# Prompt stick-breaking attention by pairs of heads, and cache pages issued by two engines

## The reference, cut to what matters

```
z[t,s] = q_t . k_s / 8 + b_h                 for s < t, else masked
beta   = sigmoid(z);  rem = sigmoid(-z) = 1 - beta
A[t,s] = beta[t,s] * prod_{s<j<t} rem[t,j]
o[t]   = sum_s A[t,s] v_s
```

## Time and profile before

| what | us |
|---|---|
| median of 3 executions | 1375.97 (1371.51 to 1376.88) |
| the profiled execution's own time | 1370.01 |
| its span in the profile | 1368.3 |
| TensorE busy in the span | 1262.4 (92%) |
| VectorE busy | 410.7 (30%) |
| ScalarE busy | 243.7 (18%) |
| GpSimd busy | 88.7 (6%) |

### The profile page before, as it was taken

The page is one execution under the profiler, slowest core; times in us unless marked ns, Lnnn a source line. Parts: engine busy times, 40 slices in busy tenths (PEclk is TensorE's granted clock), DMA queues, the critical chain, the costliest instruction groups (busy, mean ns, idle before and its releaser), DMA issues.

```text
span 1368.3 us, 19903 instructions
## 1 busy us (share of the span) xinstructions
PE 1262.4 (92%) x7806; PEld 572.1 (42%) x7806; DVE 410.7 (30%) x944; ACT 243.7 (18%) x413; POOL 88.7 (6%) x156
## 2 busy tenths in 40 slices
PE   3999996979998999999999999999999999999996
PEld 2777774559552333333333333333333333333332
DVE  1750242364362213122123212213222223212214
ACT  2214232232221101102011011101101011011103
POOL 1600122024200000000000000000000000000000
PEclk8999998889989999999999999999999999999998
DMA  9444489600255999999999999999999999999993
GB/s 324 165 128 123 136 268 369 217 21 16 112 220 201 401 429 429 429 428 428 428 428 428 429 429 429 429 428 429 428 428 429 428 428 429 428 429 429 428 426 157
DMA packets 67031, 464.11 MB, mean 339 GB/s; under 512 B 16685, under 2 KB 16813, under 8 KB 42148
## 3 DMA queue, kind: packets, MB, share of 16 engines
q1 hardware_dynamic: 64420, 455.01, 81.4%
q0 software_dynamic: 2560, 8.39, 1.7%
HBM read 459.67 MB, written 3.70 MB: 339 GB/s over the span
## 4 chain that ended last, share of the span: by engine, by line
PE 47%; DMA 21%; issue 1%; DVE 1%; SPq 1%; ACT 0%; POOLq 0%; POOL 0%; DVEq 0%; ACTq 0%
PE bank L2010 33%; DMA ring<-in_w_up 21%; PE bank L1981 4%; PE bank L1960 4%; PE bank L2031 2%; PE bank L1964 1%; PE bank L1985 1%; PE bank L2057 1%; SPq L731 0%; DVE work L2249 0%; DVE X L2244 0%; PE bank L1999 0%; PE bank L2039 0%; PE bank L2068 0%; ACT work L2124 0%
## 5 line engine op out<-in xcount | busy, mean ns | idle before, releaser
L2010 PE MATMUL bank<-ring,work 128*64 128x512 f32 x2048 | 451.4, 596 | 23.8 <-DMA ring<-in_w_up 23.8
L2010 PEld LDWEIGHTS bank<-ring,work 128*64 128x64 f32 x2048 | 149.1, 137 | 324.2 <-issue 324.2
L2031 PE MATMUL bank<-ring,work 128*64 128x512 f32 x1024 | 229.6, 597 | 10.3 <-DMA ring<-in_w_down 6.3
L2031 PEld LDWEIGHTS bank<-ring,work 128*64 128x64 f32 x1024 | 69.5, 137 | 148.7 <-issue 122.9
L432 PE MATMUL bank<-hT,ring 128*128 128x288 f32 x448 | 115.8, 414 | 11.0 <-PEq L273 10.7
L432 PEld LDWEIGHTS bank<-hT,ring 128*128 128x128 f32 x448 | 85.4, 194 | 34.0 <-issue 11.5
L2215 DVE TENSOR_SCALAR work<-bank 128x512 f32<-128x512 f32 x32 | 21.9, 685 | 257.8 <-PE bank L2010 257.8
L2108 ACT ACTIVATE work<-bank 128x1024 f32<-128x1024 f32 x16 | 16.4, 1024 | 392.6 <-PE bank L1964 392.6
L2178 DVE TENSOR_TENSOR X<-X,bank 128x512 f32<-128x512 f32 x64 | 44.0, 688 | 125.5 <-PE bank L1981 125.5
L2227 DVE COPY work<-bank 128x512 f32<-128x512 f32 x16 | 11.1, 692 | 214.6 <-PE bank L2031 214.6
L1981 PE MATMUL bank<-work 128*128 128x512 f32 x128 | 59.2, 605 | 0.0
(11 more groups left out here) (389 smaller groups left out, 1135.0 us busy)
## 6 DMA issues: line engine op xcount, KB each, us to landing
ring<-in_w_up SPq DMA_DIRECT2D x128, 2048.0 KB, 17.2
ring<-in_w_down SPq DMA_DIRECT2D x62, 2048.0 KB, 15.2
ring<-in_cache_k SPq DMA_DIRECT2D x64, 256.0 KB, 3.0
ring<-in_w_in SPq DMA_DIRECT2D x7, 2048.0 KB, 14.2
ring<-in_cache_v SPq DMA_DIRECT2D x32, 256.0 KB, 5.0
ring<-in_cache_v POOLq DMA_DIRECT2D x32, 256.0 KB, 5.0
ring<-in_w_out SPq DMA_DIRECT2D x2, 2048.0 KB, 12.7
ring<-in_w_down SPq DMA_DIRECT2D x4, 1024.0 KB, 13.9
```

The source lines that it names most:

```text
L2010: ins = pe.matmul(bank[CAP * e:CAP * e + CAP, g, :], xT[:, k, CAP * e:CAP * e + CAP], weight(ch + e, k % 2 * RSLOT + 512 * g), start=False ...
L2031: ins = pe.matmul(bank[CAP * e:CAP * e + CAP, 4 + m, :], aT[:, k, CAP * e:CAP * e + CAP], weight(ch + e, k % 4 * D + 512 * m), start=False ...
```

## The change

Prompt attention works on pairs of heads. Head a of a pair lies on one half of the partitions: `scores(p)` uses 64x64 quarters of the array, head 0 in rows and columns 0 to 63, head 1 in 64 to 127, with 64 queries at a time (chunk c) against only the 64(c+1) keys that they can see. The four chunks lie side by side in one row of 644 columns over two PSUM banks, each with one extra column of -1e30 behind it, so that beta is 0 and the remainder 1 there. The mask is added first, by a matmul of the 64x64 identity with `nS65`. One scan covers all four chunks and both heads: at each extra column `preset` holds 1 and the second operation, a maximum, resets the product to 1. Transposes are six per pair, copied by ScalarE at once (768 columns), and the value products of the two heads alternate between the array's column halves. The order of all engines is written out anew, `scores(2)` and `scores(3)` wait for the head copies of the pair two before, and the semaphores of the cache block are counted on (`DECODE_ROUNDS`). `sbp`, `nsbp` (biases by pair) and `nS65` are made by GpSimd in the projection block in place of `negS` and `nsbb`.

Cache pages: of each of the last five groups SyncE issues units 0 and 1, GpSimd units 2 and 3, the latter with two semaphores by the parity of the group; from the sixth group on GpSimd waits for its own pages of two groups before.

```diff
-        BY_POOL = (*range(16, 20), *range(24, 28))
-        s_vpool = sem("values_loaded_by_gpsimd")
+        BY_POOL = [m for m in range(12, 32) if m % 4 >= 2]
+        s_gpage = [sem(f"pages_loaded_by_gpsimd{i}") for i in range(2)]
...
+            if U_C <= u < U_WO and m in BY_POOL:
+                return eng.wait_ge(s_gpage[m // 4 % 2], 2 * PGL * 16 * ((m // 4 - 3) // 2 + 1))
...
-                pool.tensor_scalar(nsbb, sbb, -1.0, None, ALU.mult).then_inc(s_masks, 1)
+                for r, a in ((lo, 0), (hi, 1)):
+                    pool.tensor_copy(sbp[r], sbb[r, a:NH:2])
+                    c(pool.tensor_scalar(nsbp[r], sbb[r, a:NH:2], -1.0, None, ALU.mult))
+                pool.tensor_copy(nS65[:, 0:HD], nS)
+                pool.memset(nS65[:, HD:HD + 1], -BIG).then_inc(s_masks, 1)
...
-                for m in range(16, 20):
-                    load_cache(pool, m)
-                pool.wait_ge(s_vpool, 256)
-                for m in range(24, 28):
-                    load_cache(pool, m)
+                for n in range(3, 8):
+                    if n >= 5:
+                        slot_wait(pool, U_C + 4 * (n - 2) + 2)
+                    for s in (2, 3):
+                        load_cache(pool, 4 * n + s)
...
+                def scores(p):
+                    if p >= 2:
+                        pe.wait_ge(s_poe, p - 1)
+                    z = bank[:, 2 * (p % 2):2 * (p % 2) + 2, :].rearrange("p b n -> p (b n)")
+                    for c in range(4):
+                        for a in range(2):
+                            pe.matmul(z[pr(a), Z0 + ZO[c] + HD * c:Z0 + ZO[c] + HD * c + HD + 1], I64[pr(a), :], nS65[pr(a), :],
+                                      start=c in (0, 3), stop=False, skip_group_check=True)
+                    for c in range(4):
+                        for a in range(2):
+                            ins = pe.matmul(z[pr(a), Z0 + ZO[c]:Z0 + ZO[c] + HD * (c + 1)], qsT[pr(a), p, tk(c)],
+                                            ksT[pr(a), p, 0:HD * (c + 1)], start=False, stop=True, skip_group_check=True)
+                    ins.then_inc(s_pz, 1)
...
                 scores(0)
+                scores(1)
+                turn_kv(0)
+                turn(0)
+                turn_kv(1)
+                values(0)
+                turn(1)
+                scores(2)
+                turn_kv(2)
+                values(1)
+                turn(2)
+                scores(3)
+                turn_kv(3)
+                values(2)
+                turn(3)
+                turn_kv(4)
+                values(3)
...
+                def betas(p):
+                    act.wait_ge(s_pz, p + 1)
+                    if p >= 2:
+                        act.wait_ge(s_A, DECODE_ROUNDS + p - 1)
+                        act.wait_ge(s_AT, DECODE_ROUNDS + p - 1)
+                    z = bank[:, 2 * (p % 2):2 * (p % 2) + 2, :].rearrange("p b n -> p (b n)")[:, Z0:Z0 + ZW]
+                    act.activation(prem[p % 2], z, ACT.Sigmoid, scale=-SCALE, bias=nsbp[:, p:p + 1])
+                    act.activation(pbeta[p % 2], z, ACT.Sigmoid, scale=SCALE, bias=sbp[:, p:p + 1]).then_inc(s_beta, 1)
...
+                def weights(p):
+                    dve.wait_ge(s_beta, DECODE_ROUNDS + p + 1)
+                    b, m, i = pbeta[p % 2], prem[p % 2], pincl[p % 2]
+                    c(dve.tensor_tensor_scan(i[:, ::-1], m[:, ::-1], preset[:, ::-1], 1.0, ALU.mult, ALU.max))
+                    dve.tensor_tensor(b[:, 0:ZW - 1], b[:, 0:ZW - 1], i[:, 1:ZW], ALU.mult).then_inc(s_A, 1)
...
+                weights(0)
+                scale_v(0)
+                weights(1)
+                scale_v(1)
+                copy_heads(0)
+                scale_v(2)
+                weights(2)
+                copy_heads(1)
+                scale_v(3)
+                weights(3)
+                copy_heads(2)
+                scale_v(4)
+                copy_heads(3)
```

More of the change, by code:

```diff
@@ L832, in values @@
                         pe.wait_ge(s_ATe, ROUNDS[g, h])
[L833 to L837, removed]
+                        for s in range(G):
+                            slot_wait(pe, unit_of("v", g, h, s))
                         for pg in range(PGL):
@@ L1054, in turn @@
[L1054 to L1072, removed]
@@ L1074, in _ @@
-                scores(0)
-                for h in range(NH):
-                    if h + 1 < NH:
-                        scores(h + 1)
-                    turn(h)
-                    if h < 5:
-                        turn_kv(h)
-                    if h:
-                        values(h - 1)
-                values(NH - 1)
+                def scores(p):
[11 more added lines that the diff above has]
+                    ins.then_inc(s_pz, 1)
@@ new lines, in turn, with values @@
+                def turn(p):
+                    pe.wait_ge(s_A, DECODE_ROUNDS + p + 1)
+                    if p:
+                        pe.wait_ge(s_ATe, DECODE_ROUNDS + p)
+                    for i, (c, b) in enumerate(((0, 0), (1, 0), (2, 0), (3, 0), (2, 1), (3, 1))):
+                        o = ZO[c] + P * b
+                        ins = pe.transpose(bank[:, 4 + i // 4, i % 4 * P:(i % 4 + 1) * P], pbeta[p % 2][:, o:o + P], ident[:])
+                    ins.then_inc(s_AT, 1)
+                def values(p):
+                    pe.wait_ge(s_ATe, DECODE_ROUNDS + p + 1)
+                    at_ = pAT[p % 2].rearrange("p (i a q) -> p i a q", i=6, a=2)
+                    for t, rows_, q, blocks in ((0, HD, slice(0, HD), slice(0, 1)), (0, P, slice(HD, SEQ), slice(1, 4)),
+                                                (1, HD, slice(2 * HD, 3 * HD), slice(4, 5)), (1, P, slice(3 * HD, SEQ), slice(5, 6))):
+                        for a in range(2):
+                            hc = slice(HD * (2 * p + a), HD * (2 * p + a) + HD)
+                            ins = pe.matmul(bank[pr(a), 2 * (p % 2), q], vs_tok[0:rows_, t, hc], at_[0:rows_, blocks, a, :],
+                                            start=t == 0 and rows_ == HD, stop=t == 1, skip_group_check=True)
+                    ins.then_inc(s_po, 1)
```

124 lines of the change are left out of this document (54 added, 70 removed).

## The result

| what | before | after |
|---|---|---|
| median of 6 executions each | 1374.02 (1371.30 to 1376.88) | 1360.31 (1358.65 to 1365.28) |
| the profiled execution's own time | 1370.01 | 1361.68 |
| its span | 1368.3 | 1360.0 |
| TensorE busy in the span | 1262.4 | 1252.6 |
| start of the prompt stage | 252.51 | 248.25 |

The ratio after to before is 0.9904, 95% interval 0.9884 to 0.9925: faster by 1.0%, 13.7 us by the medians. The median after lies in the scatter of its own six executions, 0.2 us under the range that the prediction gave.

What follows compares the result with a forecast made beforehand. Prediction: DMA bounds the expert stage, late pages stop the cache stage, TensorE's instructions bound the prompt stage. Gains 3.9 + 3.1 = 7.0 us off 1370.0 give 1363.0, plus 6.0 to the median: 1369.0, range 1360.5 to 1377.5.

Steps and rivals of the forecast that it cites:

- Cache pages: Cache stage: one 5.2 us stop for keys replaces stops of 7.85 and 0.96 us; 3.9 us earlier, bounds 0 and 7.7.
- a term of 1 us until the semaphore: Cache stage: last keys transferred by 212.0, plus 1 us until the semaphore, so TensorE stands until 213.0.
- rival B: Cache stage: DMA is full, keys land at about 217, only the prompt's 3.1 us are left; 1373 us, chance 0.18.
- The chain of the prompt stage: Prompt stage: each pair becomes serial from scores 2, 6.8 us per pair; 27.4 us in all, 6.4 less than 33.75.
- the early fall: Prompt stage: TensorE's clock falls after scores 0, at 1.6 us, and stays low until 8.6 us, as before.
- The clock of the prompt stage: Prompt stage: low clock cuts the gain to 3.1 us; bounds 6.4 gained and 8.5 lost.
- one fall, late: Prompt stage: last turn and values take twice as long, 27.4 + 1.7 = 29.1 us.
- half of 3.1 us behind it: Delta-rule stage start: first matmuls cost up to 3.1 us more at low clock; half charged, 1.5 us.
- rival A: Clock survives the gaps: 6.4 us in the prompt stage, up to 7.7 in the cache stage; 1363.5 us, chance 0.25.
- The offset: Whole kernel: median taken as 6.0 us above the profiled execution, turning 1363.0 into 1369.0.
- The range: Whole kernel: 1360.5 to 1377.5 us, taking A whole and B with 2.7 us of scatter.
- Rival C: Slower than before: TensorE stays at 1.2 GHz through the prompt stage and into the next; 1380.6 us, chance 0.12.

Runs made afterwards that it cites:

- Pages alone: Kernel before with only the cache-page edit, prompt attention by single heads as before: 1368.38 us, ratio 0.9958 to the kernel before.
- pairs alone: Changed kernel with the cache-page edit undone, so only the prompt stage is new: 1365.44 us, ratio 0.9939 to the kernel before.
- keys page by page: Changed kernel with the last 16 key pages issued first pages first, one semaphore per two pages: 1357.06 us, ratio 0.9872 to the kernel before.

## Why the prediction came out as it did

Forecast 1369.0 us with a range of 1360.5 to 1377.5, measured 1360.31, and 1363.64 when the kernel was executed again. The gain of the profiled pair was forecast at 7.0 and is 8.3. That these two are so near is in part luck: the prompt stage gained 3.9 us more than forecast, 0.45 was there before the cache stage began, and 2.6 were given back in the delta-rule stage, 0.3 in the expert stage and 0.1 in the cache stage.

- **Cache pages: right in mechanism and size.** Forecast 3.9 us; the prompt stage starts 4.26 us earlier, of which 0.45 was there when the cache stage began (161.09, 161.54 before), so 3.8. Values ready when asked for at 203.04 as worked out, keys landed at 213.97 (213.0 forecast, with a term of 1 us until the semaphore for which no row was given), stop of 5.34 us (5.2). The clock fell behind it as it had behind the old one: 12 transposes took 2.82 us instead of 1.50. Pages alone gave 0.42%, 5.8 us by the ratio and 4.4 by the medians.
- **DMA.** The keys did not slip to 217, so rival B was wrong for this change. From 206 to 211 the transfers ran at 392 GB/s before and after, so sharing the pages between two issuers did not raise that. This agrees with the rule of the Trainium skill that transfers of all issuers share the same 16 DMA engines (DMA: Bandwidth & Descriptors, "Issuing engines are not separate DMA queues"). The rule calls the saving of a second issuer usually small; here it was worth 3.8 us, since a page of 262 KB every 1.17 us is 224 GB/s from one issuer, and the transfers ran at 392 once there were enough of them.
- **The chain of the prompt stage: right in its length, wrong in terms that partly cancel.** Forecast with a low clock in the first 8.6 us and none later 27.4 us, measured with none at all 26.8 to the end of the last head copy. Scores 2 start at 10.2 and not at 11.4, which is the early fall that did not come. Scores 1.6 us from start to start as forecast, scan 1.50 against 1.55, multiply 0.83 as forecast, sigmoids 0.80 as forecast, 6.9 us per pair against 6.8. The values took 1.33 us and not 0.75, so their halves may overlap less than assumed (not tried); the idle times were 2.07 and not 2.7, shorter by what the values were longer.
- **The clock of the prompt stage: this is the term that was mis-sized.** It made the gain of the stage 3.1 us, where 7.0 came. The prediction let it fall at the start "as now", took "one fall, late" (29.1), and half of 3.1 us behind it, so 3.1 us gained. Measured in after: no fall and nothing behind it; the stage is 7.0 us shorter, with the 3.8 and 0.45 ahead of it the 11.2 at the next stage's start. The stage begins behind work at full clock (last values 3.64 us, as the earlier trace rows had it), and whether the clock falls in it differs between executions: 1.00 throughout in after and in the pairs alone, low three times when after was executed again. In that execution the stage took 30.3 us to the end of the last head copy (29.1 forecast) with nothing behind it (1.5 forecast): 3.5 us gained, near the 3.1, so the forecast was one of the cases that occur. In the prompt stage the profiled execution of after followed rival A, which gave this a chance of 0.25. In the cache stage it did not: A counted on up to 7.7 us there, and 3.8 came.
- **A term that was missing.** 2.6 us were given back in the delta-rule stage, which the prediction carried over unchanged; 2.1 of them lie around a stretch of low clock that before did not have.
- **The offset.** The median of before stood 6.0 us above its profiled execution in the three times shown and 4.0 in six, and for after it was -1.4: the profiled execution of before was faster than all six of the timed ones, though not than all of the 41 in the experiments (1366.76 to 1380.49). That put 7.4 us into the forecast that no step accounts for. It is most of the 8.7 us between forecast and median.
- **The range.** It was said to take rival A whole, with 2.7 us of scatter. A at its most (14.1 us) is 1361.9, less 2.7 is 1359.2, but the range was written from 1360.5. The median of 1360.31 lies between the two; the working held it and the written bound did not.
- **Rival C** did not occur: none of the profiles shows 1.2 GHz through the whole prompt stage. The nearest is the kernel with keys page by page, 0.80 over its 31.6 us.

## What to carry to other kernels

When a stop of an engine goes, price two things apart: its length, and the clock behind it. The second was at least half as large as the first here (4.4 us behind stops of 5.3 and 3.4 us), and it was bought back with ten matmuls that nothing reads, where TensorE is what the end waits for; where VectorE set the pace, eight such matmuls gave nothing. And before an offset between a profiled execution and a median is added to a forecast, ask how far it is scatter of the one execution.

## What had not been expected of the hardware

The granted clock is not a function of the instructions: the same kernel, with the same idle time of 2.07 us at the same place, ran its prompt stage at 1.00 in one execution and had the clock at 0.50 in three stretches of it in another. The single-head stage fell in both its profiles (0.51 over 254 to 261 before, 0.50 over 249.8 to 256.6 with the pages alone). Of the nine profiles with pairs, in their several versions, five had a fall in the prompt stage or at its start. So one profile of each kernel doesn't show that the pairs keep the clock up. The medians of the changed kernel in two studies, 1360.31 and 1363.64, differ by about what such a fall costs; that this is the cause was not shown, and their ratios to before (0.9904 and 0.9918) agree within the intervals.
